# Other split places at mixer tails and late changes, other shares in the opening, plain down order in stage 6, and a copy ahead of the last mixer's Gelu

## The reference, cut to what matters

```python
# stages 0 to 5: twice (ffn, mixer 1, ffn), each with a modulation made from c
mod = (silu(c) @ ada_w[l] + ada_b[l]).reshape(B, 3, 3, D)     # shift, scale, gate for each sublayer
h = rmsnorm(x, norm_g) * (1 + mod[:, s, 1]) + mod[:, s, 0]
x = x + 0.5 * mod[:, s, 2] * ((silu(h @ w_gate) * (h @ w_up)) @ w_down)      # ffn, d_ff 2816
x = x + mod[:, s, 2] * ((sig(g_conv) * y_conv + sig(g_attn) * y_attn) @ w_o) # mixer 1
...
x = rmsnorm(x, final_g)                                        # behind stage 5
# stages 6 to 8: ffn, mixer 2, ffn, with a norm of the sublayer's output
h = h + 0.5 * rms_norm(swiglu(rms_norm(h, pre_g)), post_g)     # ffn
y_a = (rg_lru(causal_conv(xr)) * gelu(xg)) @ w_lru_out         # mixer 2, recurrent branch
y_b = swa_sink_attention(q, k, v) @ w_attn_out                 # mixer 2, attention branch
h = h + rms_norm((g0 * y_a + g1 * y_b) @ w_o, post_g)
```

## Time and profile before

| | us |
|---|---|
| median of 3 runs | 2157.16 (2156.02 to 2157.23) |
| profiled execution | 2157.11 |
| its span, first to last instruction | 2155.0 |
| PE busy | 2083.1 |
| DVE busy | 1415.5 |
| ACT busy | 1022.5 |
| mean granted clock of TensorE | 0.993 |

### The profile page before, as it was taken

One profiled execution on the slowest core, in us unless ns is written; L12 is line 12 of the kernel. 1 busy time (PEld: TensorE's weight loads), 2 busy tenths in 40 slices (PEclk: granted clock), 3 DMA queues, 4 the chain that ended last, 5 costly groups with the idle time before them and its releaser, 6 DMA issues.

```text
span 2155.0 us, 29736 instructions
## 1 busy us (share of the span) xinstructions
PE 2083.1 (97%) x12033; PEld 1817.3 (84%) x12033; DVE 1415.5 (66%) x1795; ACT 1022.5 (47%) x1265; POOL 36.8 (2%) x81
## 2 busy tenths in 40 slices
PE   7999999999999999999999989999999898999998
PEld 6788899999788878888999988887788787997887
DVE  5777676668687677667867776455554567656554
ACT  4443544443544363345444345435533568646343
POOL 0000000000000000000000000000000000000000
PEclk9999999999999999999999999999999899999999
DMA  9787697438587758768864575554656343456552
GB/s 310 244 285 252 191 297 227 134 120 269 191 275 252 243 179 272 234 208 266 281 165 126 191 259 195 187 184 147 210 190 195 109 131 124 157 176 200 182 194 78
DMA packets 355932, 438.09 MB, mean 203 GB/s; under 512 B 9571, under 2 KB 323371, under 8 KB 355796
## 3 DMA queue, kind: packets, MB, share of 16 engines
q1 hardware_dynamic: 350592, 420.51, 59.9%
q0 software_dynamic: 4160, 14.23, 3.0%
q10 hardware_dynamic: 1044, 1.46, 0.2%
HBM read 435.05 MB, written 1.11 MB: 202 GB/s over the span
## 4 chain that ended last, share of the span: by engine, by line
PE 78%; DVE 9%; ACT 7%; DMA 2%; DVEq 2%; issue 2%; SPq 0%; ACTq 0%
PE PC L1726 6%; PE PC L1728 6%; PE PC L1727 6%; PE PA L1726 6%; PE PA L1728 6%; PE PA L1727 6%; PE PB L1726 5%; PE PB L1728 5%; PE PB L1727 5%; PE PA L1719 4%; PE PA L1720 4%; PE PA L1721 4%; DVE lo L1132 4%; ACT hi L687 3%; PE PC L1719 2%; DVE acc L1154 2%
## 5 line engine op out<-in xcount | busy, mean ns | idle before, releaser
L1132 DVE TENSOR_TENSOR lo<-raw,hi 128x2048 fp32r<-128x2048 f32 x275 | 628.6, 2289 | 250.9 <-ACT hi L687 250.4
L687 ACT ACTIVATE hi<-raw 128x2048 fp32r<-128x2048 f32 x277 | 528.8, 1910 | 245.8 <-PE PC L1728 132.3
L1719 PE MATMUL PA<-nl,hi 128*128 128x256 f32 x976 | 283.2, 290 | 5.4 <-ACT acc L1088 3.7
L1720 PE MATMUL PA<-nh,lo 128*128 128x256 f32 x976 | 276.5, 283 | 0.0
L1721 PE MATMUL PA<-nh,hi 128*128 128x256 f32 x976 | 276.5, 283 | 0.0
L1154 DVE SCALAR_TENSOR_TENSOR acc<-raw,cs,acc 128x256 f32<-128x256 f32 x469 | 227.2, 484 | 37.4 <-issue 2.6
L1726 PE MATMUL PA<-hi,nl 128*128 128x512 f32 (+1 forms) x528 | 211.4, 400 | 14.1 <-DVE nl L1229 12.2
L1728 PE MATMUL PA<-hi,nh 128*128 128x512 f32 (+1 forms) x528 | 207.0, 392 | 0.0
L1727 PE MATMUL PA<-lo,nh 128*128 128x512 f32 (+1 forms) x528 | 206.5, 391 | 0.0
L1719 PEld LDWEIGHTS PA<-nl,hi 128*128 128x128 f32 x976 | 187.6, 192 | 8.3 <-issue 5.5
L1720 PEld LDWEIGHTS PA<-nh,lo 128*128 128x128 f32 x976 | 187.7, 192 | 0.7 <-issue 0.5
(11 more groups left out here) (293 smaller groups left out, 3849.0 us busy)
## 6 DMA issues: line engine op xcount, KB each, us to landing
raw<-in_w_in SPq DMA_DIRECT2D x90, 1024.0 KB, 6.3
raw<-in_ada_w SPq DMA_DIRECT2D x70, 1024.0 KB, 7.3
raw<-in_ffn_w_gate SPq DMA_DIRECT2D x88, 512.0 KB, 4.1
raw<-in_ffn_w_up SPq DMA_DIRECT2D x88, 512.0 KB, 5.2
raw<-in_ffn_w_down SPq DMA_DIRECT2D x44, 1024.0 KB, 5.1
raw<-in_ffn_w SPq DMA_DIRECT2D x88, 512.0 KB, 4.8
raw<-in_ffn_w SPq DMA_DIRECT2D x22, 1024.0 KB, 5.0
raw<-in_w_o SPq DMA_DIRECT2D x12, 1024.0 KB, 6.2
```

Source lines behind the costliest of these rows:

```text
L687: A(parts_of(n)[0], raw[:, n % 3, :], ACT.Copy).then_inc(hi_done, 1)
L1132: V.tensor_tensor(l, raw[:, n % 3, :], h.bitcast(F32), ALU.subtract).then_inc(lo_done, 1)
L1719: MM(o, wh[:, c0:c0 + w], xl, start=first, stop=False, skip_group_check=True)
L1720: MM(o, wl[:, c0:c0 + w], xh, start=False, stop=False, skip_group_check=True)
```

## The change

- Opening: DVE makes unit 3 too, between units 2 and 4; PE makes only 1 and 6, the latter behind the fold of unit 4. SP's waits for slots follow.
- Stage 0: the modulation unit of group 1 is made behind the low part of group 0.
- Mixer tails: `w3` takes the third w_o unit. In the last step ACT splits it before it waits for PE, and the fourth behind that wait, ahead of `mH`; DVE takes the third one's low part between the sum and `mL`.
- All changes: DVE makes the first two low parts of the normed x between its evictions of four chunks (`apply`, `lows`), the other two behind them, where before all four stood behind.
- Changes behind stages 5 and 7: ACT splits the third unit right behind the last high part, then come both tiles' statistics and Silu's table; DVE has the low part ahead of the reciprocals.
- Stage 6: down products in plain order, `slot_tables` and `finished` to match; ACT and DVE split one unit more ahead, PE's transposes of x behind the last down product.
- Stage 7: ACT copies Gelu's bank (`gc_done` releases it) at the head of the step, and Gelu works in place; `chunk_T` stands before the recurrent gates and before `lru` on ACT, and inside `conv2` on DVE.

```diff
@@ finished, slot_tables
-    if STAGES[s] != "ffn" or not LATE <= k <= LATE + 2:
+    if STAGES[s] != "ffn" or s == 6 or not LATE <= k <= LATE + 2:
...
-            if kind == "ffn" and k % 4 == 3 or kind != "ffn" and k == UNITS[kind] - 1:
+            if kind == "ffn" and k % 4 == 3 or kind != "ffn" and k == UNITS[kind] - 2:
@@ ACT, change: s == 5 (s == 7 the same way)
                     final_stats(1)
+                    apply(Aq, 1)
+                    split(BASE[s + 1] + 2)
                     next_stats(s, 0)
-                    apply(Aq, 1)
                     next_stats(s, 1)
-                    behind()
+                    A(spare[:, :], eps[:, 0:1], ACT.Silu)
@@ ACT, ffn
+                if s == 6:
+                    split(b + 32)
                 hidden(NG - 2)
-                split(b + 32)
+                split(b + (33 if s == 6 else 32))
...
                 if s < 8:
-                    split(b + 33)
+                    split(b + (34 if s == 6 else 33))
@@ ACT, tail
+                    if last:
+                        split(b + n + 3)
                     after(b + n)
+                    if last:
+                        split(b + n + 4)
...
-                    split(b + n + 3)
+                    if not last:
+                        split(b + n + 3)
                 A(spare[:, :], eps[:, 0:1], ACT.Sqrt)
-                split(b + len(units) + 3)
@@ ACT, stage 7
             def gelu(j):
-                after(b + 3 + (2, 5, 8, 11)[j])
-                if j:
-                    act.wait_ge(lru_v, 6 * j - 1)
-                A(gl, prod[(1, 0, 1, 0)[j]], ACT.Gelu_apprx_tanh).then_inc(gl_done, 1)
+                act.wait_ge(gc_done, j + 1)
+                A(gl, gl, ACT.Gelu_apprx_tanh).then_inc(gl_done, 1)
...
+                if i == 4 and 0 <= j < 4:
+                    after(b + 3 + u)
+                    if j:
+                        act.wait_ge(lru_v, 6 * j - 1)
+                    A(gl, prod[(1, 0, 1, 0)[j]], ACT.Copy).then_inc(gc_done, 1)
                 if t is not None:
                     tick(2, 32, 0, t, STEPS)
+                if c is not None:
+                    chunk_T(8 + c, c, oH2)
@@ DVE, apply
                     if c % 2:
                         i.then_inc(ud_done, 1)
+                        lows(Aq, t, (c // 2 - 2,))
                 dve.drain()
-                lows(Aq, t, range(4))
+                lows(Aq, t, (2, 3))
@@ DVE, tail
+                        if n == len(units) - 1:
+                            split(b + n + 3)
                         dve.wait_ge(mH_done, n0 + j + 1)
@@ DVE, opening
-            for n, u in enumerate((0, 2, 4, 5, 7)):
+            for n, u in enumerate((0, 2, 3, 4, 5, 7)):
@@ DVE, ffn
                     split(b + 3 * i + 2)
                     low(i - 1)
+                    if i == 1 and first is not None:
+                        ada(mid[i])
@@ DVE, conv2
                 V.tensor_copy(cpad[:, :, 4:], ...).then_inc(cp_done, 1)
+                if c is not None:
+                    chunk_T(8 + c, c, oH2, oL2)
@@ PE, ffn
-                        for t in range(1 if i == NG - 2 else 2):
+                        for t in range(1 if i == NG - 2 and s != 6 else 2):
...
-                for n in range(4):
+                for n in range(2 if s == 6 else 0, 4):
...
                 down(i, 1, 0)
+                down(i, 1, 1)
                 if s == 6:
                     turn_x(s + 1, 0)
-                down(i, 1, 1)
@@ PE, opening
-            for n, u in enumerate((0, 2, 4, 5, 7)):
-                if n < 2:
-                    ada_cols_of(2 * n + 1)
+            for n, u in enumerate((0, 2, 3, 4, 5, 7)):
                 if n == 0:
+                    ada_cols_of(1)
                     rows_turned()
-                if n == 3:
+                if n == 4:
                     ada_cols_of(6)
@@ PE, bank_free
-                    pe.wait_ge(gl_done, (u - 2) // 3 + 1)
+                    pe.wait_ge(gc_done, (u - 2) // 3 + 1)
```

More of the change, by code:

```diff
@@ L117, in slot_tables @@
             last[c] = n
-            free[c] = n + 3.5 if kind == "ffn" and k == LATE else n
+            free[c] = n + 3.5 if kind == "ffn" and k == LATE and s != 6 else n
             raws[n % 3] += 32 if is_up(s, k) else 16
@@ L389, in build @@
         rs_done = sem("rs_done")
+        gc_done = sem("gc_done")
         mod_done, mods_rdy = sem("mod_done"), sem("mods_rdy")
@@ L505, in load_ada @@
                 if n == 0:
-                    sp.wait_ge(ada_d, 5)
+                    sp.wait_ge(ada_d, 6)
                 else:
@@ L567, in _ @@
                 c = u % 4
[L568 to L572, removed]
+                if u == 5:
+                    sp.wait_ge(ada_p, 1)
+                elif u >= 4:
+                    sp.wait_ge(ada_d, (1, 0, 2, 3)[c])
                 sp.dma_start(raw[:, c, :].rearrange("p (k f) -> p k f", k=KC),
@@ L797, in change @@
                     apply(Aq, 1)
-                    between()
                     behind()
@@ L890, in tail @@
                 for n, (kind, j) in enumerate(units):
+                    last = n == len(units) - 1
                     if n == 0:
                         per_chunk()
+                    if last:
+                        split(b + n + 3)
                     after(b + n)
+                    if last:
+                        split(b + n + 4)
                     if kind in ("ga", "gc"):
@@ L1098, in _ @@
                     lru(j - 1, 1)
-                if c is not None:
-                    chunk_T(8 + c, c, oH2)
                 if i == 4 and 0 <= j < 4:
@@ L1303, in change @@
                     final_norm(1)
+                    apply(Aq, 1)
+                    behind()
                     recip(("n", Aq, 0))
-                    apply(Aq, 1)
                     recip(("n", Aq, 1))
@@ L1318, in change @@
                     apply(Aq, 1)
-                    split(BASE[s + 1] + 1)
                 elif s == 7:
@@ L1332, in change @@
                         add_postnorm(s, t)
-                if s < 8:
+                if s < 5 or s == 6:
                     behind()
@@ L1366, in ffn @@
                 for i in range(1, NG - 1):
-                    ada(mid[i])
+                    if i > 1 or first is None:
+                        ada(mid[i])
                     split(b + 3 * i + 2)
                     low(i - 1)
+                    if i == 1 and first is not None:
+                        ada(mid[i])
                     split(b + 3 * i + 3)
@@ L1468, in tail @@
                         dve.wait_ge(mL_done, n0 + j + 1)
-                    split(b + n + 3)
+                    if n < len(units) - 1:
+                        split(b + n + 3)
                 split(b + len(units) + 3)
             dve.wait_ge(cs_done, 1)
-            for n, u in enumerate((0, 2, 4, 5, 7)):
-                if n == 2:
+            for n, u in enumerate((0, 2, 3, 4, 5, 7)):
+                if n == 3:
                     dve.wait_ge(rowsT, 1)
                     V.tensor_copy(vec[:, :], PA[:, 0:384]).then_inc(vec_done, 1)
-                if n == 4:
+                if n == 5:
                     normed(0, 0)
@@ L1590, in early @@
                 def early():
-                    split(BASE[s + 1])
+                    split(BASE[s + 1] + 1)
                     late()
@@ L1681, in _ @@
                 if i == 0 and 0 <= j < 4:
-                    conv2(j)
+                    conv2(j, c)
                 if i == 4 and 0 <= j < 4:
@@ L1688, in _ @@
                     lru(j - 1, 2)
-                if i != 3 and c is not None:
+                if i == 0 and j == 4 and c is not None:
                     chunk_T(8 + c, c, oH2, oL2)
```

8 lines of the change are left out of this document (4 added, 4 removed).

## The result

| | before | after |
|---|---|---|
| median, us | 2157.19 | 2140.27 (2139.34 to 2144.5) |
| profiled execution | 2157.11 | 2139.62 |
| its span | 2155.0 | 2137.8 |
| ratio, 95% interval | | 0.9925 [0.9907, 0.9942] |

A forecast was written before the change was run, and what follows sets the result against it. PE (TensorE) was taken as the bound, busy 2083.1 of 2155.0 us, so at most 72 us of idle could be won. Terms summed to -20.2, plus 4.8 for new falls: 2157.1 to 2141.7 us, range 2138 to 2146.

The forecast's parts named there:

- cL wait: Stage 0: PE's idle 1.9 us for the first hidden low part goes once the modulation unit stands behind it; -1.8 us.
- Tails: Mixer tails of stages 1, 4, 7: earlier w_o splits shorten them by 2.7, 1.1 and 1.2; together -5.0 us.
- Changes behind 5 and 7: Behind stages 5 and 7: earlier third-unit split ends a 2.3 us wait and clock fall; 2.8 each, -5.6 us.
- Low parts: All changes: low parts between evictions bring PE's second tile 0.4 us earlier, kept in stages 0, 1, 4, 7; -1.6 us.
- Stage 6: Plain order: first tile's transposes unmoved, high and low parts follow at once, stage 7 starts earlier; -5.3 us.
- Loop of stage 7: Gelu and oL waits go, but PE waits 2.4 us for the convolution; three rounds, -2.2 us.
- Rival (c): Stage 7: emptied Gelu bank does nothing, the convolution's chain is the bound; 2143.9 us; chance 0.55 together with the forecast.
- Falls: New idle runs in stages 1, 4 and 7 bring three clock falls at 1.6 us each; +4.8 us.
- (a): Whole kernel: the clock holds at the new waits; 2136.9 us, with far bounds 2134.5; chance 0.17.
- (b): Tails, stage 6, low parts: waits only move, through late landings, counting cover and no low-part gain; 2149.4 us; chance 0.18.
- (d): Whole kernel within 0.2% of before: (b) and five falls in stage 7; 2154 us; chance 0.06.
- (e): Stage 7's loop: clock stays low through it, kernel slower; some 2185 us, threshold case 2158 to 2165; chance 0.04.

## Why the prediction was right, point by point

- **Opening.** Right in size and mechanism: the first matmul stands 1.6 later, expected 1.3. What I had only as a bound is real: unit 3's landing now sets it (landed 19.88, transposes of x at 37.82; in the run with the low parts behind, 18.72 and 36.66). In the eleven profiles with the new shares the first transposes of x stand between 36.55 and 37.91, in the three with the old ones between 36.19 and 36.37. The mean cost is 1.1. An earlier landing than 18.6 brought nothing: 17.52 gave 36.55, 18.64 gave 36.58.
- **cL wait.** Right (-2.1 for -1.8); no later low part of the stage came late.
- **Tails.** The mechanism was right to the instruction: the fourth split waits for its load, and mH, mL and the low part behind it. Waits 1.46 and 2.94 were forecast as 1.8 and 2.3. The last was mis-sized by the landing, 6.2 us where I had taken 5.4 from before. What I missed in stage 1 is a wait of 1.6 before the first w_o part, where 0.4 stood: two small waits ahead of it are gone, and the split of that unit still stands behind mH. It costs little: in the two runs with the opening's old shares the small waits are back and this one is 0.5, and PE reaches the part only 0.2 to 0.3 earlier for it.
- **Changes behind 5 and 7.** Right in sum, with a new wait of 1.3 for my 0.9. The undoing showed that more than half of it (1.6 of 2.9) hangs on a clock fall.
- **Low parts.** The step that failed, though the total hides it: in the term of -1.6 I let the 0.4 of stage 7 stand, and in stages 2, 3 and 5 I took the gain as swallowed, no more. It is -0.8: 0.4 in three stages, nothing in stage 7, and 0.1 lost in each of 2, 3 and 5.
- **Stage 6.** Right: transposes at the same time, the first matmul 4.7 earlier in the span's offsets (forecast 4.6), all of it behind them. The further 0.7 goes with the fall at 1709, which didn't come back; I had said that the clock was low either way.
- **Loop of stage 7.** Right: 29.4 us a round with a wait of 2.65 for 2.4. Rival (c) says that the emptied bank does nothing, and the undoing shows just that; with falls counted the copy costs 2.2. As a time (2143.9) it took the whole loop term away, and the chunk order kept that. The loop came out 1.1 better than forecast, since the first round won 1.1 and not 0.7, and a fall in a round cost 1.2 (30.55 beside 29.38) and not 1.6.
- **Falls.** Three at 1.6 each was the right count, at three of the five places named. That is in part luck: it was an average over idle runs and named no place, and another execution of the same kernel took 2144.5 with a mean clock of 0.992 instead of 0.995, which by 1.6 each is an estimate of three falls more. Rivals (a) and (b) are out (no new falls; waits only move), (d) with them, and so is (e): the loop stays at 1.00 but for single falls.
- **The pages.** The table load at both changes takes 1.28 in the kernel after too, with ACT's next instruction 0.01 behind it (1508.40 to 1509.69), and the changes came out at 2.9 and 2.8. So the 2.7 us of the Trainium skill ("ScalarE: Activation LUTs", introduction) doesn't show in this trace and would have spoiled that step. The Trainium skill's rule on the clock ("TensorE: Matmul & The Clock Gate", Terms), half of the throttled time, gives 0.31 x 5.50 = 1.7 us for the fall behind stage 7 in the run with the changes undone, and 1.6 was measured there (2.9 less 1.3). For the fall in the third round it gives 0.05 x 30.55 = 1.5 us, and 1.2 was measured (30.55 beside 29.38). So it fits where PE waits for nothing behind the fall, and is too dear where a wait behind the fall takes up part of it.

## What to carry to other kernels

Where two traces share their instructions, subtract the times of the same matmul in both: each stretch then shows its own gain, far below what total times resolve. In a loop through several engines, ask which engine's work shortens the round when some is taken away; the busy share didn't tell it here, and moving a wait along the same queue brought nothing. And two waits of 1.2 us can be cheaper than one of 2.65, so an edit that merges waits has to be priced with the clock.

## What the runs showed of the hardware

In all fourteen profiles, behind the first 75 us, PE has 54 idle runs of 2.2 to 3.9 us that begin at full clock; 45 are followed by a fall to 1.2 GHz. Of 125 between 1.0 and 2.2 there are 9, of 102 between 0.7 and 1.0 one. The same matmul with the same wait had the clock at 1.00 in the kernel before (2.83) and at 0.79 in the one with its tails and opening (2.80), and of the waits of 2.65 to 3.0 in stage 7's rounds five of seven in the first round passed without a fall, of those in the second and third two of fourteen. What tells these apart stays open; no run here shows it. The record of the granted clock also misses the start: the first twelve matmuls of stage 0 stand 0.43 us apart in the kernels before and after, where later ones of their size stand 0.23 apart, and the record has 1.00 over them.
